# Taking up a V row three turns behind its U row, in place of two, in a decoder step with gathered experts

## What is computed

```
q = (hb @ w_q).reshape(PEER_BLOCK, PEER_HEADS, 2, PEER_KEY_DIM // 2)
sc = jnp.einsum('thpd,hpnd->thpn', q, sub_keys)
s1, i1 = lax.top_k(sc[:, :, 0], PEER_TOPK)
s2, i2 = lax.top_k(sc[:, :, 1], PEER_TOPK)
...
e = i1 * N_KEYS + i2                      # 8 heads x 16 experts for each token
gate = jax.nn.softmax(top_s, axis=-1)
act = jax.nn.gelu(jnp.einsum('thkd,td->thk', u_tab[e], hb), approximate=False)
return jnp.einsum('thk,thkd->td', gate * act, v_tab[e])
```

## Time and profile before

| | |
|---|---|
| median of three runs | 3372.73 us (3368.57 to 3376.57) |
| span of the profiled execution | 3372.4 us |
| PE / DVE / ACT / POOL busy | 88% / 67% / 47% / 39% of the span |
| mean granted TensorE clock | 0.959 |
| moved by DMA | 1298.74 MB, 1140.92 MB of it by the gathers' queue |
| chain that ended last | PE 44%, DMA 28%, DVE 20%, ACT 4% |

### The profile page before, as it was taken

One profiled execution on the slowest core, in us unless ns is written; L12 is line 12 of the kernel. 1 busy time (PEld: TensorE's weight loads), 2 busy tenths in 40 slices (PEclk: granted clock), 3 DMA queues, 4 the chain that ended last, 5 costly groups with the idle time before them and its releaser, 6 DMA issues.

```text
span 3372.4 us, 34890 instructions
## 1 busy us (share of the span) xinstructions
PE 2967.9 (88%) x10654; PEld 1563.0 (46%) x10654; DVE 2247.2 (67%) x5353; ACT 1569.5 (47%) x4312; POOL 1299.0 (39%) x1097
## 2 busy tenths in 40 slices
PE   7988899988999898989898888998897988798877
PEld 5764556653445444554454333443353434353322
DVE  1268737685678647884779568866777486873854
ACT  2137334555456334643456345644563454432433
POOL 0023324344344434443434444453334443343532
PEclk8998999999999999999999999999999998899999
DMA  4279999999999999999999999999999989999998
GB/s 175 91 298 362 387 386 396 418 394 421 421 420 411 421 422 419 393 405 422 421 400 413 421 422 421 410 421 422 396 382 408 422 351 333 353 393 369 421 422 342
DMA packets 241250, 1298.74 MB, mean 385 GB/s; under 512 B 46068, under 2 KB 70804, under 8 KB 100646
## 3 DMA queue, kind: packets, MB, share of 16 engines
q0 software_dynamic: 156672, 1140.92, 82.5%
q1 hardware_dynamic: 84390, 155.59, 12.4%
HBM read 1279.41 MB, written 16.44 MB: 384 GB/s over the span
## 4 chain that ended last, share of the span: by engine, by line
PE 44%; DMA 28%; DVE 20%; ACT 4%; issue 2%; SPq 1%; POOL 0%; DVEq 0%; ACTq 0%
PE PS L1096 21%; DMA R<-in_t_uv,idx 18%; DVE R L1746 8%; PE PS L779 7%; DMA R<-in_t_uv,idxS 4%; DMA wring<-in_w_out 3%; PE PS L745 2%; PE PS L1018 2%; PE PS L860 2%; PE PS L859 2%; DVE xb L1757 2%; DMA wring<-in_w_query 2%; PE PS L1045 2%; DVE SC L1712 1%; DVE SC L1709 1%
## 5 line engine op out<-in xcount | busy, mean ns | idle before, releaser
L1096 PE MATMUL PS<-R,diag 128*128 128x512 f32 x3776 | 1821.4, 619 | 200.3 <-ACT diag L1378 173.6
L710 POOL DMA_INDIRECT R<-in_t_uv,idx x1024 | 1234.3, 1205 | 1949.1 <-PE PS L1096 1389.3
L1746 DVE CUSTOM_DVE_ANT_0 R<-R,hb 128x1024 f32<-128x1024 f32 x1088 | 1315.7, 1220 | 726.4 <-DMA R<-in_t_uv,idx 645.3
L1096 PEld LDWEIGHTS PS<-R,diag 128*128 128x128 f32 x3776 | 694.6, 195 | 1077.5 <-issue 635.4
L1369 ACT ACTIVATE acts<-dots 128x1 f32<-128x1 f32 x1088 | 217.2, 200 | 1103.1 <-DVE dots L1746 1100.4
L1378 ACT ACTIVATE diag<-ident,wv 128x128 f32<-128x128 f32 x880 | 353.7, 402 | 76.9 <-PE PS L1096 49.0
L779 PE MATMUL PS<-R 128*128 128x128 f32 (+2 forms) x2272 | 317.1, 295 | 38.6 <-ACT stg L1140 26.7
L779 PEld LDWEIGHTS PS<-R 128*128 128x128 f32 x2272 | 298.5, 196 | 113.1 <-issue 104.5
L1371 ACT ACTIVATE wv<-gate,acts 128x1 f32<-128x1 f32 x1024 | 301.9, 295 | 33.3
L1757 DVE SCALAR_TENSOR_TENSOR xb<-R,wv,xb 128x1024 f32<-128x1024 f32 x144 | 184.4, 1281 | 1.7 <-ACT wv L1371 1.7
L1018 PE MATMUL PS<-wring,T 128*128 128x512 f32 x256 | 133.0, 649 | 42.6 <-DMA wring<-in_w_out 42.6
(11 more groups left out here) (243 smaller groups left out, 2376.0 us busy)
## 6 DMA issues: line engine op xcount, KB each, us to landing
wring<-in_w_out SPq DMA_DIRECT2D x64, 512.0 KB, 14.0
wring<-in_w_query SPq DMA_DIRECT2D x64, 512.0 KB, 8.1
R<-in_t_win SPq DMA_DIRECT2D x38, 512.0 KB, 8.5
R<-in_t_uv,idx POOLq DMA_INDIRECT x1024, 14.0
R<-in_t_win SPq DMA_DIRECT2D x9, 1024.0 KB, 16.0
pr<-prd SPq DMA_DIRECT2D x8, 976.0 KB, 12.7
prd<-stg SPq DMA_DIRECT2D x54, 128.0 KB, 7.6
xb<-in_x_prompt SPq DMA_DIRECT2D x8, 512.0 KB, 7.9
```

The lines of the kernel that those rows point to most:

```text
L710: e.indirect_dma_start(dst, None, table, bass.IndirectOffsetOnAxis(ap=index, axis=0)).then_inc(S[s], c.count(name, s, 16))
L1096: m = mm(bank(n), diag[:, NTH[s] % DR, :], pair(s)[:, D + 512 * n:D + 512 * n + 512], start=begins, stop=s == last_slot(t), skip_group_che ...
L1746: e.tensor_tensor_reduce(u, u, hb[:, tile_of(g) % 2, :], 1.0, 0.0, ALU.mult, ALU.add, dots[:, g % NW:g % NW + 1]).then_inc(dve_done, c.cou ...
```

## The change

`LAG` is 3 in place of 2. It stands in five places: the number of turns, TensorE's V rows, VectorE's V rows, and the turns of `ysum`, its square, the scaling, the store and the next load at a tile's end. Items, U rows, ScalarE's slot work and the gathers keep their turns; what the gathers wait for keeps its name, but is now issued a turn later.

```
-LAG = 2
+LAG = 3
```

## The result

The median is 3381.54 us (ten runs, 3375.66 to 3389.25) against 3370.12 us for the kernel before (ten runs, 3366.91 to 3376.57): ratio 1.003, 95% interval 1.0019 to 1.0040. The change makes the kernel slower by 0.3%, some 10 us. The profiled execution of the changed kernel is the slowest of its ten (span 3387.5 us), so its rows show 15 us more than before where the medians show 11, and I read from it where something happens and take the size from the ratios.

The account below looks back on a forecast made before the run. Transfers were taken to bound the long saturated stretches, with other limits between, such as TensorE from 400 to 710 us. Terms of +12 - 3 - 7 = +2 us on a span of 3372.4 gave 3375 us, 8-in-10 range 3359 to 3398.

Parts of the forecast that it names:

- What bounds the kernel: Transfers limit 710 to 1400 and 1745 to 2420 us; from 400 to 710 us TensorE is busy for 302.90 of 310.
- The saturated windows at nothing: From 710 to 1400 and 1745 to 2420 us, the queue of gathers hides homes that come free later: cost nothing.
- The six ends: Where transfers rule again after five stretches and a w_query slab wait, late homes cost 2 us each: +12 us (7 to 15).
- VectorE's V rows: 144 rows in attention move behind one more U row and its items; no cost beyond the +12 us for late homes.
- Waits that go: TensorE's waits for the diagonal before V rows, mainly in the decode pages from 2715 to 2960 us: -3 us (-8.5 to 0).
- The tile's start: TensorE's scores no longer stand behind the wait for ysum, 5 us in tile 7 and 2 elsewhere: -7 us (-12 to 0).
- ScalarE at 0: ScalarE, preparing diagonals one V row ahead of TensorE instead of two, waits more, at no cost while TensorE is behind.
- rival (c): ScalarE is chained to TensorE: its 49.0 us of waits double, half on attention's path, +24 us: 3397 us; chance 0.08.
- Rival (a): Ring too short with 8 or 9 homes, seven page waits from 2715 to 2960 us: 3405 or 3391 us; chance 0.28.
- Rival (b): TensorE's waits were the bound, in tile 7 and the decode stretch: 3359 us, or 3366 at half; chance 0.22.
- these shares: DMA shares to watch: 1.01 from 1900 to 2400 us; from 2715 to 2960 us 0.90 for the forecast.
- the two gains: The forecast's negative terms: -3 us for TensorE's waits for the diagonal and -7 us for the wait for ysum.

Follow-up runs that it names:

- e9: Three turns for slots 128 to 775 only, two elsewhere, on both engines, against the kernel before: 3383.75 us, ratio 1.0035.
- e7: Three turns from slot 776 on only, two before it, against the kernel before: 3375.91 us, ratio 1.0017.
- e2: Changed kernel with VectorE's V rows back at two turns, TensorE's at three; against the kernel before: 3382.14 us, ratio 1.0022.
- e3: Kernel before with three turns for VectorE's 144 V rows only; against the kernel before: 3386.16 us, ratio 1.0037.
- e6: Kernel before with only each tile's first V row on TensorE (tiles 2 to 9) a turn later: 3373.92 us, ratio 1.0008.
- e1: Changed kernel with five diagonals in place of four and PP cut to 1040 columns; against the kernel before: 3402.38 us, ratio 1.0085.
- e4: Kernel before (two turns) with one home fewer in the ring, 8, 10 and 7 homes: 3389.46 us, ratio 1.0053.
- e10: Four turns everywhere and on both engines (LAG = 4), against the kernel before: 3445.66 us, ratio 1.0216.
- e11: Three turns for TensorE's V rows of tile 1 only, two for all else, against the kernel before: 3362.53 us, ratio 0.9967.
- e12: Three turns only 21 to 96 slots into a tile, within slots 128 to 775; against the kernel before: 3376.66 us, ratio 1.0005.

## Why the prediction was right and wrong

I gave 3375 us and a range of 3359 to 3398, with 0.42 on no measurable change. The time lies in the range, on the side to which I gave 0.36. One row of the kernel before, of line L710 from 710 to 1400 us, goes with the second point:

```profile
DMA to landing us min/median/max: 8.5/15.9/24.6
```

Point by point:

- **What bounds the kernel** held: transfers in long stretches, TensorE in 400 to 710 us.
- **The saturated windows at nothing: this step failed in the first of the two.** I took 8.4 us, the least time to landing less a turn's items, over a floor of 5.5 as cover. But I had read it from 1900 to 2400 us, where the ring has 11 homes, and carried it over to 710 to 1400 us, where it has 9. There the row above has a median of 15.9 us, not 21.0. Where it was read, it holds: slots 560 to 768 take 569.0 us in place of 566.6 (all kernels 564.4 to 569.4). Even 8.5 less 1.4 would be over 5.5, so there is a second fault in it. What a V row stands behind isn't a turn's *busy* time of 1.4 us, but an item with its wait, 3.98 us and then 3.75 us at a lower clock at 956 us. The mean of a turn doesn't price the turns in which an item waits. The runs show 0.35% for the slots 128 to 775 (e9), most of which I had at nothing.
- **The six ends at 2 us each**, 12 us: about the size of the whole loss, but not its form, and so by luck. It isn't spread over the ends of stretches. The late part costs 5.7 us (e7), and about 6 us of transfers are lost at one place, behind a page 11.57 us late.
- **VectorE's V rows**, in the price of the ends and not beside it: that the two don't add up fits (e2, e3), but alone these rows cost 0.37% (e3), as much as all six ends together, and the count of ends doesn't explain that.
- **Waits that go, -3 us**: the wait for the diagonal fell to 95.3 us, under the 120 that I gave. It is worth nothing that the runs show, since the waits for items grew by 60 us (41.8 for L1140, 18.0 for L1415) against 78 that went.
- **The tile's start, -7 us: failed in the sum.** Its signs came in part: the wait for `ysum` fell from 25.5 to 10.8 us over the program, in tile 7 from 5.53 to 2.00, but in tile 9 it grew from 3.34 to 5.80. e6 puts the time at 1.0008 (0.9993 to 1.0024): at best 2 us of the 7. I had counted a wait off the path of the transfers as if it were on it.
- **ScalarE at 0, and rival (c)**: its wait did more than double (49.0 to 113.6 us), as (c) says, yet freeing it gives nothing back (e1).
- **Rival (a)**, a ring too short, is nearest to what the runs show, by e4 and e10, where the ring has 8 or 9 homes, but not in the way that I gave it: the share from 2715 to 2960 us is 0.91, where I had asked for 0.87 or less, and it happens at one page, not at seven. The test was too coarse.
- **Rival (b)** shows in tile 1, and no run shows it elsewhere. There TensorE is the bound, and e11 keeps the gain.
- I wrote that I would be wrong if the time moved by over 0.2% with these shares unchanged. That is what happened. The time to landing can't be read from 1900 to 2400 us in the changed kernel's trace; GpSimd's and VectorE's waits there don't replace it, so that sign stays open.

The sum would have been right in sign with the two gains at nothing: 3372.4 + 12 = 3384 us. That would have been luck as well: the 12 us were put at other places, and the upper part of my range came from (a)'s page waits and from (c), which e1 refutes.

**What stays open**: why the page lands late. In the changed kernel SyncE's issue of one page before it takes 5.73 us, where 0.33 is usual; in e1, e7 and e10 one takes 5.1 to 5.7 as well. In e2 and e3 the longest is 1.1 and 2.8 us, and the page is late all the same. From the last issue for that sequence to the end of TensorE's wait it is 14.0 to 15.7 us in the six kernels with a third or fourth turn there, 13.1 in e4, and 8.0 to 10.4 in the six others that wait for it (10.1 before): once issued, the page lands later, too, and why isn't shown. Open is also whether the price in the middle is the late home or the waiting item; e12 speaks for the item, e4, e10 and the 11 homes for the ring.

## What to carry to other kernels

Moving a step back by a turn in an in-order queue doesn't remove a wait, it chooses what stands behind it: look for the items that wait for another engine, not for the mean length of a turn, and ask which held buffer is released behind them. A deep queue of transfers on average (a share of 1.01) says little about a ring; take one buffer away and see, read the time to landing in each stretch that has a ring size of its own, and compare kernels from slot to slot, not in windows at fixed times. Set such a distance by stage: here three turns where TensorE is the bound, two where the ring has 8 or 9 homes; with 11 the third turn shows no price.

## What had not been expected

- A fifth diagonal with `PP` cut to 1040 columns costs 0.31%, though ScalarE's wait falls to 8.7 us and no instruction is added.
- No stretch of 10 us in the fourteen traces, begun at any whole microsecond, moved more than 431 GB/s, at shares of 1.02 and 1.03; the two long saturated windows of the kernel before moved 417 and 418. The Trainium skill's page Perfetto Trace Analysis (Roofline) puts the limit of a core's 16 DMA engines at about 435 GB/s; the best 10 us lie 1% under it.
- Two pairs of matmul groups show what a wait does to the same work. In the changed kernel the 16 transposes of L745 on a page take 3.67 us behind 11.57 us of waiting; 16 of the same shape take 1.97 us at 2850.44 us, without a wait. The 16 of L779 take 3.75 us behind 3.98 us of waiting, and 1.95 us without, in the kernel before.
